# A dense selection table: one block's eight units built by matmul ahead of the loop, 24 units scattered as before, two of them beside the build

## The reference, cut to what matters

```python
s = jnp.einsum('thpd,hpnd->thpn', q, sub_keys)          # two lists of 128 key scores
s_top, i_top = lax.top_k(s, PEER_TOPK)                  # 16 best of each
cand = s_top[:, :, 0, :, None] + s_top[:, :, 1, None, :]
c_top, c_idx = lax.top_k(cand.reshape(...), PEER_TOPK)  # 16 best pairs
expert = idx1 * PEER_KEYS + idx2                        # idx1, idx2 in 0..127
gate = jax.nn.softmax(c_top, axis=-1)
u = u_table[eb]
hid = jax.nn.gelu(jnp.einsum('td,thkd->thk', xb, u)) * gb
out = jnp.einsum('thk,thkd->td', hid, v_table[eb])
```

## Time and profile before

| | us |
|---|---|
| median of 3 runs (3672.59 to 3676.25) | 3674.01 |
| profiled execution | 3676.73 |
| its span | 3675.0 |

### The profile page before, as it was taken

One profiled execution on the slowest core, in us unless ns is written; L12 is line 12 of the kernel. 1 busy time (PEld: TensorE's weight loads), 2 busy tenths in 40 slices (PEclk: granted clock), 3 DMA queues, 4 the chain that ended last, 5 costly groups with the idle time before them and its releaser, 6 DMA issues.

```text
span 3675.0 us, 36366 instructions
## 1 busy us (share of the span) xinstructions
PE 3377.6 (92%) x10816; PEld 1902.7 (52%) x10816; DVE 2663.1 (72%) x6220; ACT 926.6 (25%) x2312; POOL 2061.8 (56%) x1618
## 2 busy tenths in 40 slices
PE   7999997995998899495699999999999999999998
PEld 4666774574565677352244444444444444444443
DVE  2476664385798787324388889878988888888888
ACT  3244443211233344221011121112112121112212
POOL 1000000087888788788566666656665666565665
PEclk9999997997998899697799999999999999999999
DMA  4454113144432333342799999999999999999998
GB/s 122 155 205 162 58 39 131 49 104 82 69 53 24 52 53 36 79 86 6 258 400 384 390 394 375 379 358 397 376 375 394 388 387 375 386 387 380 371 408 326
DMA packets 370772, 868.60 MB, mean 236 GB/s; under 512 B 97552, under 2 KB 192016, under 8 KB 363408
## 3 DMA queue, kind: packets, MB, share of 16 engines
q0 software_dynamic: 221184, 537.23, 43.2%
q1 hardware_dynamic: 126976, 243.06, 18.2%
q10 hardware_dynamic: 22416, 85.99, 5.9%
HBM read 828.14 MB, written 38.01 MB: 236 GB/s over the span
## 4 chain that ended last, share of the span: by engine, by line
PE 48%; DMA 2%; DVE 1%; issue 1%; POOL 0%; ACT 0%; ACTq 0%; DVEq 0%; POOLq 0%
PE peer_ps_o L2053 24%; PE peer_ps_d L2040 21%; PE peer_ps_q L2003 2%; DMA peer_vr<-in_v_rows,index_g 1%; DMA peer_ur<-in_u_rows,index_g 0%; DVE Y L2201 0%; PE peer_ps_s L2013 0%; POOL peer_ur L1970 0%; DVE peer_ur L2190 0%; POOL peer_vr L1978 0%; DVE Y L2218 0%; PE peer_ps_t L2022 0%; DVE Y L2177 0%; ACT xg L2077 0%; DVE wk L2218 0%
## 5 line engine op out<-in xcount | busy, mean ns | idle before, releaser
L1420 POOL DMA_INDIRECT sel<-lists x512 | 834.5, 1630 | 290.1 <-issue 152.5
L1970 POOL DMA_INDIRECT peer_ur<-in_u_rows,index_g x512 | 566.6, 1107 | 519.6 <-DVE peer_ur L2190 396.0
L2201 DVE SCALAR_TENSOR_TENSOR Y<-peer_vr,osq,Y 128x1024 f32<-128x1024 f32 x512 | 657.1, 1283 | 93.5 <-DMA peer_vr<-in_v_rows,index_g 93.2
L1978 POOL DMA_INDIRECT peer_vr<-in_v_rows,index_g x512 | 599.1, 1170 | 195.7 <-issue 148.7
L2190 DVE SCALAR_TENSOR_TENSOR peer_ur<-peer_ur,Y 128x1024 f32<-128x1024 f32 x512 | 629.6, 1230 | 93.5 <-DMA peer_ur<-in_u_rows,index_g 93.5
L2053 PE MATMUL peer_ps_o<-hw,Y 128*128 128x512 f32 x1024 | 447.9, 597 | 8.4 <-DVE Y L2177 8.4
L2053 PE MATMUL peer_ps_o<-hnT,Y 128*128 128x512 f32 x1024 | 442.6, 592 | 0.0
L2040 PE MATMUL peer_ps_d<-hnT,state 128*128 128x512 f32 x688 | 303.9, 595 | 78.0 <-PEq L1455 78.0
L2053 PEld LDWEIGHTS peer_ps_o<-hw,Y 128*128 128x128 f32 x1024 | 196.1, 192 | 251.5 <-issue 238.9
L2053 PEld LDWEIGHTS peer_ps_o<-hnT,Y 128*128 128x128 f32 x1024 | 193.6, 190 | 238.7 <-issue 238.7
L2040 PE MATMUL peer_ps_d<-hnT,held 128*128 128x512 f32 x688 | 302.4, 592 | 0.7 <-ACT Y L2083 0.7
(11 more groups left out here) (335 smaller groups left out, 4910.3 us busy)
## 6 DMA issues: line engine op xcount, KB each, us to landing
sel<-Y ACTq DMA_DIRECT2D x16, 2048.0 KB, 7.0
peer_mt<-sel ACTq DMA_DIRECT2D x64, 512.0 KB, 7.6
hw<-in_v_cols SPq DMA_DIRECT2D x16, 2048.0 KB, 10.4
hnT<-in_v_cols SPq DMA_DIRECT2D x16, 2048.0 KB, 13.2
state<-in_u_cols SPq DMA_DIRECT2D x43, 512.0 KB, 7.1
held<-in_u_cols SPq DMA_DIRECT2D x43, 512.0 KB, 7.3
peer_ut<-in_u_cols SPq DMA_DIRECT2D x42, 512.0 KB, 7.3
w_group<-in_w_ssd SPq DMA_DIRECT2D x32, 512.0 KB, 4.1
```

Source lines behind the costliest of these rows:

```text
L1420: nc.gpsimd.indirect_dma_start(sel.rearrange("a i q two (t o) -> (a i q two t) o", o=1), bass.IndirectOffsetOnAxis(ap=R.index_d[:, at, k:k ...
L1970: nc.gpsimd.indirect_dma_start(ur[:, r % RING, :], None, u_rows, bass.IndirectOffsetOnAxis(ap=R.index_g[:, r // TOPK % RQ, r % TOPK:r % TO ...
L1978: nc.gpsimd.indirect_dma_start(vr[:, r % RING, :], None, v_rows, bass.IndirectOffsetOnAxis(ap=R.index_g[:, r // TOPK % RQ, r % TOPK:r % TO ...
L2201: nc.vector.scalar_tensor_tensor(out=hb, in0=vr[:, s, :], scalar=hid[:, c:c + 1], in1=hb, op0=ALU.mult, op1=ALU.add).then_inc(comb_done, 1)
```

## The change

Of the 32 dense units, the 8 of block 3 (`BUILT`, units 17, 19, ... 31) are no longer scattered. `route_place` only stores their expert numbers as floats. At the start of `peer` a build makes their part of `sel`. The expert numbers and gates are turned by PE, so that partitions are a token's 128 choices (8 heads by 16 ranks) and columns are the 128 tokens. DVE compares a row 0..127 with the first key of each choice (`hot_a`) and with the second, times the gate (`hot_b`); for the last of every four tokens ACT makes the second by an Abs and a Relu. A matmul of the two is that token's 128 by 128 piece of the table. Groups of 4 tokens go through two buffers each; ACT copies each product in two halves to staging buffers (`place_out`), and SP stores them to `sel`, in pieces of 512 bytes, 2.1 MB for each of four staging buffers. The rest (24 units) is scattered as before, but in another split: 4 units in mix0, 3 ahead of ssd1's chunks, 5 in them (5 launches per chunk), 8 in hg1, 2 in mix1, and 2 by POOL in `peer`, behind the first five row gathers. ACT, POOL and SP get waits for the stores.

```diff
-DENSE = [n for n in range(UNITS) if n // (2 * PH) * 2 + n % 2 < DB]
+SCATTERED = [n for n in range(UNITS) if n // (2 * PH) * 2 + n % 2 < DB - 1]
+BUILT = [n for n in range(UNITS) if n // (2 * PH) * 2 + n % 2 == DB - 1]
+DENSE = SCATTERED + BUILT
...
-SCATTER_MIX0, SCATTER_PROLOGUE, SCATTER_SSD = DENSE[0:5], DENSE[5:8], DENSE[8:15]
-SCATTER_CHUNK = 7
-SCATTER_HG, SCATTER_MIX1 = DENSE[15:25], DENSE[25:]
+SCATTER_MIX0, SCATTER_PROLOGUE, SCATTER_SSD = SCATTERED[0:4], SCATTERED[4:7], SCATTERED[7:12]
+SCATTER_CHUNK = 5
+SCATTER_HG, SCATTER_MIX1, SCATTER_BUILD = SCATTERED[12:20], SCATTERED[20:22], SCATTERED[22:]
+M_GROUPS = P // 4
+PER_BATCH = SELB // 4
...
# route_place
+    if n in BUILT:
+        nc.vector.tensor_copy(R.built_key[:, ...], chosen).then_inc(R.routed, 1)
+        return
...
# peer, SP, ahead of the load of va
+            for x in range(4):
+                batch, hh, parts = x // 2, x % 2, stage_parts(x)
+                sp.wait_ge(staged, 2 * (PER_BATCH * (batch + 1) - 1) + hh + 1)
+                to = sel[:, hh * 32:(hh + 1) * 32, (DB - 1) * P // SELB + batch].rearrange("a i two t -> a i (two t)")
+                for i in range(parts):
+                    bs = slice(i * 4 // parts, (i + 1) * 4 // parts)
+                    sp.dma_start(to[:, i * 32 // parts:(i + 1) * 32 // parts, :], ...).then_inc(sel_out[x // 2], 16)
+            sp.wait_ge(sel_out[0], sel_stores(0))
             sp.dma_start(va, v_cols[0, 0]).then_inc(v_in[0], 16)
...
# peer, POOL
+            nc.gpsimd.iota(count_u, ...).then_inc(M.counted, 1)
             for r in range(RING):
                 u_row(r)
+            for n in SCATTER_BUILD:
+                scatter(nc, pool, R, sel, n, range(TOPK))
+            pool.wait_ge(sel_out[1], sel_stores(1))
             for r in range(RING):
                 v_row(r)
...
# peer, PE, ahead of the slots
+            pe.wait_ge(split_done, 1)
+            for i, part in enumerate((first_key, R.built_key, R.built_gate)):
+                mm = nc.tensor.transpose(ps_t[:, i, :], part, C["ident"][:])
+            mm.then_inc(pick_turned, 1)
+            for j in range(M_GROUPS):
+                pe.wait_ge(hot_ready, 2 * (j + 1))
+                pe.wait_ge(last_ready, 2 * (j + 1))
+                need(pe, staged, 2 * (j - 1))
+                for q in range(4):
+                    mm = nc.tensor.matmul(ps_o[:, j % 2, q * P:(q + 1) * P], hot_a[j % 2][:, q, :], hot_b[j % 2][:, q, :],
+                                          start=True, stop=True)
+                mm.then_inc(sel_made, 1)
+            pe.wait_ge(staged, 2 * M_GROUPS)
...
# peer, ACT: hot_last(j) is an Abs, a wait for it and a Relu, 128 wide; place_out(j, hh) copies 4 x 64 columns
+                act.wait_ge(last_ready, 2 * j + 1)
...
             def gelu(e):
                 act.wait_ge(s_made, e + 1)
+                if e == 0:
+                    act.wait_ge(sel_out[1], sel_stores(1))
...
+            hot_last(0)
+            hot_last(1)
+            for j in range(M_GROUPS):
+                place_out(j, 0)
+                if j + 2 < M_GROUPS:
+                    hot_last(j + 2)
+                place_out(j, 1)
-            for b in range(DB):
+            for b in range(DB - 1):
                 act.wait_ge(R.scattered[b], 16 * TOPK * PH)
+            for batch in range(2):
+                act.wait_ge(sel_out[batch], sel_stores(batch))
             load_sel(0)
...
# peer, DVE: hot(j) is one is_equal of 4 x 128 columns and three is_equal-times-gate of 128; it waits for sel_made of group j - 2
+            own.now(nc.vector.tensor_scalar(first_u, R.built_key, 1.0 / KEYS, 0.5 / KEYS - 0.5, ALU.mult, ALU.add))
+            own.now(nc.vector.tensor_copy(first_key, first_u))
+            nc.vector.scalar_tensor_tensor(out=R.built_key, in0=first_key, scalar=-float(KEYS), ...).then_inc(split_done, 1)
+            dve.wait_ge(M.counted, 2)
+            nc.vector.tensor_copy(count, count_u).then_inc(split_done, 1)
+            for j in range(M_GROUPS):
+                hot(j)
-            for b in range(DB):
+            for b in range(DB - 1):
                 dve.wait_ge(R.scattered[b], 16 * TOPK * PH)
```

More of the change, by code:

```diff
@@ L1276, in __init__ @@
             sem("best_ready"), sem("gates_ready"), sem("routed"), sem("gated"))
-        self.scattered, self.negated = [sem(f"scattered{b}") for b in range(DB)], sem("negated")
+        self.scattered, self.negated = [sem(f"scattered{b}") for b in range(DB - 1)], sem("negated")
         self.u_in = [sem(f"u_in{i}") for i in range(UT)]
@@ L1838, in _, with peer @@
                 route_gates(nc, dve, R, n)
-def peer(nc, w_route, u_cols, v_cols, u_rows, v_rows, fin_w, sel, C, Y, osq, hw, hnT, R, ut, out):
+def peer(nc, M, w_route, u_cols, v_cols, u_rows, v_rows, fin_w, sel, C, Y, osq, hw, hnT, R, ut, out):
     with ExitStack() as ctx:
@@ L1860, in peer @@
         mt = sb("mt", [P, 2, PAIR])
+        mflat = mt[:].rearrange("p s c -> p (s c)")
+        hot_a, hot_b = ([mflat[:, side * PAIR + i * 4 * KEYS:side * PAIR + (i + 1) * 4 * KEYS].rearrange(
+            "p (q c) -> p q c", q=4) for i in range(2)] for side in range(2))
+        pickedT = vr[:, RING - 1, 0:4 * P].rearrange("p (i t) -> p i t", t=P)
+        count, first_key = vr[:, RING - 1, 4 * P:5 * P], vr[:, RING - 1, 5 * P:6 * P]
+        count_u, first_u = vr[:, RING - 1, 6 * P:7 * P].bitcast(U32), vr[:, RING - 1, 7 * P:8 * P].bitcast(U32)
         fss, frs, dots, act_out, hid = osq[:, 0, :], osq[:, 1, :], osq[:, 4, :], osq[:, 5, :], osq[:, 6, :]
@@ L1870, in peer @@
         vb = hnT[:, 1].rearrange("p k c -> p (k c)").rearrange("p (e d) -> p e d", e=GE)
+        stage = [hw[:, 0:4 * D].rearrange("p (b d) -> p b d", d=D),
+                 hnT[:, 1].rearrange("p k c -> p (k c)").rearrange("p (b d) -> p b d", d=D),
+                 Y[:, 0:4, D:MIX], vr[:, 0:4, :]]
         wk, qs, xg = R.wk, R.qs, R.xg
@@ L1892, in peer @@
         fw_in = sem("fw_in")
+        split_done, pick_turned, pick_out = sem("split_done"), sem("pick_turned"), sem("pick_out")
+        hot_ready, sel_made, staged, last_ready = sem("hot_ready"), sem("sel_made"), sem("staged"), sem("last_ready")
+        sel_out = [sem(f"sel_out{i}") for i in range(2)]
         x_turned, x_out = sem("x_turned"), sem("x_out")
@@ L2219, in norm, with hot @@
                                                op0=ALU.mult, op1=ALU.mult).then_inc(f_normed, 1)
-            for b in range(DB):
+            def hot(j):
+                if j == 0:
+                    dve.wait_ge(pick_out, 1)
+                need(dve, sel_made, j - 1)
+                t = j * 4
+                nc.vector.tensor_tensor(hot_a[j % 2], count.unsqueeze(1).to_broadcast([P, 4, KEYS]),
+                                        pickedT[:, 0, t:t + 4].unsqueeze(2).to_broadcast([P, 4, KEYS]),
+                                        ALU.is_equal).then_inc(hot_ready, 1)
+                for q in range(3):
+                    ins = nc.vector.tensor_scalar(hot_b[j % 2][:, q, :], count, pickedT[:, 1, t + q:t + q + 1],
+                                                  pickedT[:, 2, t + q:t + q + 1], ALU.is_equal, ALU.mult)
+                ins.then_inc(hot_ready, 1)
+            own = R.own
+            own.now(nc.vector.tensor_scalar(first_u, R.built_key, 1.0 / KEYS, 0.5 / KEYS - 0.5, ALU.mult, ALU.add))
+            own.now(nc.vector.tensor_copy(first_key, first_u))
+            nc.vector.scalar_tensor_tensor(out=R.built_key, in0=first_key, scalar=-float(KEYS), in1=R.built_key,
+                                           op0=ALU.mult, op1=ALU.add).then_inc(split_done, 1)
+            dve.wait_ge(M.counted, 2)
+            nc.vector.tensor_copy(count, count_u).then_inc(split_done, 1)
+            dve.wait_ge(split_done, 2)
+            for j in range(M_GROUPS):
+                hot(j)
+            for b in range(DB - 1):
                 dve.wait_ge(R.scattered[b], 16 * TOPK * PH)
@@ L2290, in block_program @@
                     hnT, R, ut)
-        peer(nc, w_route, u_cols, v_cols, u_rows, v_rows, fin_w, sel, C, Y, osq, hw, hnT, R, ut, out)
+        peer(nc, M, w_route, u_cols, v_cols, u_rows, v_rows, fin_w, sel, C, Y, osq, hw, hnT, R, ut, out)
 def laid_out(inputs):
```

37 lines of the change are left out of this document (added).

## The result

The changed kernel takes 3592.01 us (median of 4 runs, 3590.30 to 3593.85), the kernel before 3673.30 beside it: a ratio of 0.9777, 95% interval 0.976 to 0.9794. That is 81 us less. The forecast was 3608 with a range from 3594: right in its direction and in the mechanism of its largest terms, 16 us too slow, and 2 us outside its range. The profiled execution has a span of 3588.5 us.

A forecast was written before the change was run, and what follows sets the result against it. The prediction saw three holes where other engines wait for POOL to launch scatters, beside a loop bound by PE and DMA. 3676.7 - 122.3 - 3 + 59.3 = 3610.7 profiled, 3608 median; range 3594 to 3636.

The forecast's parts named there:

- The three holes: Ends of mix0, hg1, mix1: engines wait 26, 32 and 67 us for POOL's scatters; gains 25.0, 31.0 and 66.3 us.
- The fear that POOL keeps its 3.7 to 6.5 us at the edges: Stage edges: if POOL kept this delay though it isn't last, 13 us of the 122.3 gain would go.
- ssd1: Stage ssd1: with 5 launches per chunk in place of 7, DVE sets the pace; gain 3 us, bounds 0 and 16.
- hg1: Stage hg1: 31.0 us from its end; the skipped address instructions of built units there counted at nothing.
- ssd1 was bound by POOL after all: Rival in ssd1: the 16 us of PE's waits come back, giving 3595; chance 0.03.
- The build: Start of peer: POOL's scatters are the later chain, done 73 us in; the loop starts 59.3 us later in the stage.
- After that: Loop from PE's third tile to the end: no change, 0 us, with bounds of -5 and +6.
- late stores: Rival in peer: slow groups and 33 us of stores are the late chain, 3634; chance of a late build 0.11.
- table loads in the build: Rival in peer: ACT changes tables between Abs and Relu in every group, 3688; 0.06, shared with another build twice as long.
- the starved POOL: Rival in peer: DVE starves the scatters, each launch waiting for a 0.69 us instruction, 22 us more, 3630; chance 0.14.

The follow-up runs named there:

- e2: The changed kernel with 7 launches per chunk in ssd1, as before, and 6 units in hg1 in place of 8; 3603.6 us.
- e7: The changed kernel with DVE's address instructions given back to the three built units routed in hg1 alone, result unused; 3598.2 us.
- f3: The changed kernel itself measured once more, with no edit; 3591.0 us.
- e1: The changed kernel with the two units scattered beside the build moved to mix1 (4 units there, none in the build); 3580.5 us.
- e5: e1 with one semaphore per staging buffer, so that the loop's start waits for half of the stores; 3584.0 us.
- e9: e5 with 4 launches per chunk in ssd1, 5 units in mix1 and va's load between the stores of buffers 1 and 2; 3593.8 us.
- e10: e9 with 3 launches per chunk in ssd1 and the unit left over scattered beside the build; 3596.0 us.
- f1: The changed kernel with 4 launches per chunk in ssd1, 4 units in mix1 and one beside the build; 3580.9 us.
- e12: e6 with va's load issued between the first and second half of the stores; 3586.4 us.
- e6: The changed kernel with the two units beside the build taken from two different blocks, so POOL doesn't wait between them; 3592.2 us.
- e3: The changed kernel with DVE's five address instructions given back to each of the eight built units, result unused; 3597.5 us.
- e4: The kernel before, without the build, with the changed split in mix0, ssd1 and hg1 and the other 12 units in mix1; 3749.8 us.

## Why the prediction came out as it did

- **The three holes** were right: mix0 and mix1 within 0.6 us, with DVE last in each and 0.33 to 0.63 us between the stages. The fear that POOL keeps its 3.7 to 6.5 us at the edges didn't come true where it ends early.
- **ssd1 is the step that failed**, and hg1, below, is as large a miss. The prediction says of ssd1 that "DVE had hardly a hole, so this wait was mostly no loss", and takes 3 "nearest DVE's own work". The gain was 12.3 (e2: 11.8 of it are the launches), out of 17.5. The reading compared two busy shares, 277 and 286 of 333, and left out the 45.9 us between launches, which the waits of POOL list and the busy time doesn't; with them POOL had no slack, while DVE stood idle for 47 of the 333. And DVE's own busy time was partly awide in its way (282.5 us in e2, 267.1 after; 7.5 of the difference are the ssd_xc instructions). That DVE then sets the pace fits PE's waits in the changed kernel. The rival "ssd1 was bound by POOL after all", given 0.03, was the right one in kind. The Trainium skill's page "Perfetto Trace Analysis", section "Identifying the Most-Contended Engine", ranks Vector, Scalar and GPSIMD by occupancy; here that named DVE of the three, and the runs say POOL.
- **hg1**: "Those in hg1 I count at nothing" was wrong by some 7 of the 10 us that the term was short (291.3 to a mean of 284.5): the address work of three units makes DVE late where PE waits for it, and in e7 that work alone brings 292.2 back. The other 3 are the changed kernel's first profiled execution, which f3 doesn't repeat.
- **The build** was short by 6.1 us. The late chain was POOL's, as said, and the build's own was done near its 71 (the last store's issue at 1690.24 and 14.0 us to landing: 69). But the wait between the units was 6.4, just above the bound of 6.2, and not the 1.2 taken: it ended 46.9 us into peer, 1.2 us behind the landing of the first half of the stores. The first 16 launches came every 2.1 us beside DVE, not 1.99 (by turns 1.6 and 2.0 us long); the last 16, most of them with DVE idle, every 1.85 (1.55 long). ACT's Gelu brought a table load of 1.28 that the sum didn't have. That the two units stand here and not in mix1 was priced at 2 us; e1 gains 11.5.
- **After that**, 0 taken, -5 to +6 as bounds: -7.5. In the kernel before, PE waited in the loop's first 60 us, as this line of its timeline shows:

```profile
1853.93 23.42 PE L2053 MATMUL peer_ps_o<-hw,Y 128*128 128x512 f32 x50 [3.67 <-DVE Y L2177]
```

  The changed kernel does the same sums without a wait. That more is in place when its loop starts is the likely reason, but no run isolates it.

```profile
1765.72 27.63 PE L2109 MATMUL peer_ps_o<-hw,Y 128*128 128x512 f32 x64
```

  Up to PE's second block of sums with the second table the loop is 5.0 us shorter (82.1 to 77.1 from the third tile; 78.6 in f3). The other 2.5 lie at its end, where kernels with the same build differ by 5 (rest: 1872.1 to 1877.6), so they can't be given to the change. A much earlier start gives part back: up to the same point e5, e9 and e10 take 84.3 to 86.9. For e1 and f1 (79.2 and 79.7, and a rest within that spread) it is hardly clear of the noise.
- The rivals of late stores and table loads in the build did not occur: no table load stands between Abs and Relu, and PE's groups came every 1.4 us, at a granted clock of 1.00 from 8.5 us into peer on. Of the starved POOL only the 0.1 us per launch above came true, not a wait of 0.69.

Four terms missed by 6 to 10 us. Three of them were gains taken at or near nothing, 27 us in all; the build, a loss taken too small, hid 6 of these by luck. The result lies 2 us outside the range, so by this sum any one of the three, put right, would have brought it in.

## What to carry to other kernels

Before an engine is called slack in a stage, add the gaps between its own instructions to its busy time and look at what it waits for: an engine that waits for nobody may be the bound though another has the larger share. A microsecond of work that is taken off an engine counts at each place where another engine waits for it, and more where PE's clock falls behind the wait. Work that is moved beside transfers is priced with its landing, not its launch; ask which large load stands ahead of it in the queues.

## What the runs showed of the hardware

A scatter's landing depended on the loads issued ahead of it: 3.1 us or 7.7 for the same launch (e12, e6). Stores in 512-byte pieces, 4.2 MB, took 17 us from the first issue to the last landing in e1, some 245 GB/s, with va's load issued 6 us behind the first. Behind a PE wait of 2 us the granted clock fell to the 1.2 GHz level for 6.8 us in three traces (before, e3, e7) and not in a fourth (e4). An ssd_xc on DVE, with two SBUF inputs, that met an `awide` on POOL ended 0.56 us behind it, 2.2 to 2.7 us long in place of 0.75 (before); beside a launch it kept its 0.75.
